# Moving the first block's gated recurrence from stages of its own into the stage of its input projections

## The reference, cut to what matters

```python
u = rmsnorm(h, mix_norm[l])
p = u @ w_mix_in[l]                       # 1024 -> 3712 columns (29 tiles of 128)
p_conv, p_hg, p_rw = jnp.split(p, ...)    # 6, 12 and 11 tiles
y = concatenate([short_conv_mixer(p_conv), hgrn2_mixer(p_hg), rwkv7_mixer(p_rw)])
```

```python
b = cumsum(log_f)                         # inside a chunk
o_inter = (q * exp(b)) @ state            # what came before the chunk
att[t, s] = sum_d q[t,d] k[s,d] exp(b[t,d] - b[s,d])   for s <= t
o = o_inter + att @ v
state = exp(b_last) * state + (k * exp(b_last - b)).T @ v
```

## Time and profile before

| | |
|---|---|
| median of 3 runs | 3573.84 us |
| fastest and slowest | 3562.53 and 3575.74 us |
| span of the profiled execution | 3556.9 us |
| time of the profiled execution beside its span | not given apart; the fastest run is 5.6 us, the median 16.9 us above the span |
| TensorE busy | 3365.1 us (95%) |
| VectorE busy | 1915.8 us (54%) |
| ScalarE busy | 1191.7 us (34%) |
| mean granted clock of TensorE | 0.971 |

### The profile page before, as it was taken

The page is one execution under the profiler, slowest core; times in us unless marked ns, Lnnn a source line. Parts: engine busy times, 40 slices in busy tenths (PEclk is TensorE's granted clock), DMA queues, the critical chain, the costliest instruction groups (busy, mean ns, idle before and its releaser), DMA issues. The chain is left out here.

```text
span 3556.9 us, 49475 instructions
## 1 busy us (share of the span) xinstructions
PE 3365.1 (95%) x21386; PEld 2766.5 (78%) x21386; DVE 1915.8 (54%) x2703; ACT 1191.7 (34%) x1678; POOL 5.5 (0%) x6
## 2 busy tenths in 40 slices
PE   7999996799999999999997799999999988999998
PEld 5888885778788888888886778788887857878886
DVE  4434656755454445444647655453456766457475
ACT  3322433134332233223423033332233175334243
POOL 0000000000000000000000000000000000000000
PEclk9999997899999999999996899999999999999999
DMA  3323222014123232323220023122323202323232
GB/s 122 110 85 105 93 89 66 2 52 134 60 95 101 95 101 89 107 89 104 89 88 10 3 67 130 66 95 96 100 95 119 89 1 91 117 72 106 90 99 73
DMA packets 78200, 301.73 MB, mean 85 GB/s; under 512 B 8946, under 2 KB 9586, under 8 KB 77344
## 3 DMA queue, kind: packets, MB, share of 16 engines
q1 hardware_dynamic: 77984, 298.56, 25.4%
HBM read 296.40 MB, written 6.06 MB: 85 GB/s over the span
## 5 line engine op out<-in xcount | busy, mean ns | idle before, releaser
L315 DVE TENSOR_TENSOR w_lo<-ring,w_hi 128x1024 fp32r<-128x1024 f32 (+1 forms) x508 | 652.8, 1286 | 503.1 <-ACT w_hi L308 503.1
L333 PE MATMUL ps<-xa_hi,w_hi 128*128 128x512 f32 x1728 | 686.3, 397 | 14.2 <-DVE w_lo L315 12.6
L334 PE MATMUL ps<-xa_lo,w_hi 128*128 128x512 f32 x1728 | 677.7, 392 | 0.0
L335 PE MATMUL ps<-xa_hi,w_lo 128*128 128x512 f32 x1728 | 677.4, 392 | 0.0
L308 ACT ACTIVATE w_hi<-ring 128x1024 fp32r<-128x1024 f32 (+1 forms) x508 | 554.1, 1099 | 336.4 <-DMA ring<-in_ffn_in_dram 74.7
L333 PE MATMUL ps<-xb_hi,w_hi 128*128 128x512 f32 x1248 | 490.1, 393 | 0.0
L335 PE MATMUL ps<-xb_hi,w_lo 128*128 128x512 f32 x1248 | 486.4, 390 | 0.0
L334 PE MATMUL ps<-xb_lo,w_hi 128*128 128x512 f32 x1248 | 486.3, 390 | 0.0
L333 PEld LDWEIGHTS ps<-xa_hi,w_hi 128*128 128x128 f32 x1728 | 327.1, 189 | 94.0 <-DVE w_lo L315 14.7
L334 PEld LDWEIGHTS ps<-xa_lo,w_hi 128*128 128x128 f32 x1728 | 327.5, 190 | 68.8 <-issue 3.0
L335 PEld LDWEIGHTS ps<-xa_hi,w_lo 128*128 128x128 f32 x1728 | 327.1, 189 | 68.9
(11 more groups left out here) (356 smaller groups left out, 3485.0 us busy)
## 6 DMA issues: line engine op xcount, KB each, us to landing
ring<-in_ffn_in_dram SPq DMA_DIRECT2D x176, 512.0 KB, 3.5
ring<-in_ffn_out_dram SPq DMA_DIRECT2D x64, 704.0 KB, 4.1
ring<-in_mix_in_dram SPq DMA_DIRECT2D x58, 512.0 KB, 3.5
ring<-in_up_dram SPq DMA_DIRECT2D x44, 512.0 KB, 3.5
ring<-in_w_in_dram SPq DMA_DIRECT2D x22, 512.0 KB, 3.5
ring<-in_down_dram SPq DMA_DIRECT2D x16, 704.0 KB, 4.1
ring<-in_mix_out_dram SPq DMA_DIRECT2D x16, 512.0 KB, 3.6
ring<-in_xk_dram SPq DMA_DIRECT2D x16, 512.0 KB, 3.4
```

The source lines that it names most:

```text
L315: dve.tensor_tensor(core.w_lo[j][:, 0:width], core.ring[j][:, 0:width], core.w_hi[j][:, 0:width].bitcast(F32), ALU.subtract).then_inc(self ...
L333: pe.matmul(out, hi, x_hi, start=(opens and k == tiles[0]), stop=False)
L334: pe.matmul(out, hi, x_lo, start=False, stop=False)
L335: last = pe.matmul(out, lo, x_hi, start=False, stop=(closes and k == tiles[-1]))
```

## The change

The three stages of `hgrn` are gone. Their work is put into steps 9 to 26 of the projection stage, by a class `Recurrence` whose `tensor`, `scalar` and `vector` are called at the end of each step, on banks 4 to 7 alone. Its buffers `u[6]` to `u[8]` lie where the ring's slots 3 and 4 lay; the projection blocks use only slots 0 to 2, are split two steps ahead, and use banks 0 to 2; bank 3 takes the three low-rank products, one before each of the projections 23, 24 and 25. The order of the tiles is forget, query, input, convolution, gate. The level buffers are two in place of three. The memset of the picked matrix is on GpSimd. The outputs from the states accumulate onto those from inside the chunks in PSUM, without chunk 0, whose state is zero. The convolution moves to steps 16 to 22 and works in place. The copy of two tiles of y moves to the start of `rwkv`, and so does, in layer 0, the DMA of the bias rows. The small weights `g2` are loaded early in the projection stage.

```diff
-ORDER = [*range(HF, HF + 3), *range(CONV0, CONV0 + 6), *range(HQ, HQ + 3), *range(HI, HG + 3), RWA, RG,
+ORDER = [*range(HF, HF + 3), *range(HQ, HQ + 3), *range(HI, HI + 3), *range(CONV0, CONV0 + 6), *range(HG, HG + 3), RWA, RG,
          *range(RK, RK + 3), *range(RR, RR + 3), *range(RV, RV + 3)]
...
 class Stream:
     def add(self, part):
         part.first = len(self.plan)
-        self.plan += part.blocks
+        for block in part.blocks:
+            last = {j: max((n for n, at in enumerate(self.slot) if at == j), default=j - RING) for j in range(part.slots)}
+            j = min(last, key=last.get)
+            self.before.append(last[j])
+            self.slot.append(j)
+            self.plan.append(block)
...
 class MixIn(Project):
+    slots, AHEAD, LORA = 3, 2, 3
...
     def sync(self, sp, n):
...
+        if n == self.first + 4:
+            sp.wait_ge(self.phase["used"], self.first)
+            sp.dma_start(self.lora_g, self.io["g2"][self.layer]).then_inc(self.phase["lora"], 16)

     def tensor_all(self, pe):
         for i in range(self.n):
-            if i >= 4:
-                pe.wait_ge(ph["projected"], self.base + i - 3)
+            if i >= 3:
+                pe.wait_ge(ph["projected"], self.base + i - 2)
...
+            if 23 <= i < 26:
+                m = i - 23
+                if m == 0:
+                    pe.wait_ge(ph["squashed"], 1)
+                    pe.wait_ge(ph["lora"], 32)
+                else:
+                    pe.wait_ge(ph["opened"], m)
+                pe.matmul(core.ps[:, self.LORA, :], ...).then_inc(ph["low_rank"], 1)
             ph.stream.multiply(pe, self.first + i, KD, self.x, core.ps[:, self.bank(i), :], ready)
             self.rooted(pe, i)
+            self.recurrence.tensor(pe, i)
...
-            self.phase.stream.split_hi(act, self.first + i + LEAD)
+            if i:
+                self.split_hi(act, i + self.AHEAD)
             self.scalar_aside(act, i, link)
+            self.recurrence.scalar(act, i)
...
-        if i == 12:
-            self.projected(act, 11)
+        if i == 9:
+            self.projected(act, 5)
             act.activation(self.q, self.q, ACT.Silu).then_inc(ph["q_silu"], 1)
...
+class Recurrence:
+    TURN_V, TURN_K, SCORES, UPDATES, INSIDE, ACROSS = 9, 10, 11, 12, 24, 25
+
+    def level(self, i):
+        n, late = divmod(i - self.SCORES, 2)
+        return (n, late) if 0 <= n <= len(LEVELS) else (None, None)
+
+    def tensor(self, pe, i):
+        ph, ps = self.phase, self.core.ps
+        if i in (self.TURN_V, self.TURN_K):
...
+            for q in range(4):
+                if n:
+                    pe.wait_ge(ph["h_copied"], q + 1)
+                for m in range(3):
+                    last = pe.transpose(ps[:, 4 + q, m * P:(m + 1) * P], self.moves[n][0][:, m, q * P:(q + 1) * P], ...)
+                last.then_inc(ph["h_turned"], 1)
+        n, late = self.level(i)
+        if n is not None and not late:
+            if n == 0:
+                pe.wait_ge(ph["h_copied"], 8)
+                pe.wait_ge(ph["q_silu"], 1)
+            else:
+                pe.wait_ge(ph["h_formed"], 2 * n)
+                pe.wait_ge(ph["h_picked"], 4 * n)
+            if n == 1:
+                pe.wait_ge(ph["h_taken"], 4)
+            for m, h, c in SYSTEMS:
+                last = pe.matmul(by_head(ps, 4, m, h, c), ...)
+            last.then_inc(ph["h_scored"], 1)
+        if i == self.UPDATES:
+            pe.wait_ge(ph["h_picked"], 4)
+            chunk_updates(pe, ps, ph["h_updated"], self.ke_n, self.v_n, 4)
+        if i == self.INSIDE:
+            pe.wait_ge(ph["h_picked"], 4 * (len(LEVELS) + 1))
...
+        if i == self.ACROSS:
+            pe.wait_ge(ph["h_inside"], 1)
+            for m in range(3):
+                pe.wait_ge(ph["h_carried"], m + 1)
+                for c in range(1, NCH):
+                    for h in range(2):
+                        last = pe.matmul(self.out_at(m, h, c), ..., start=False, ...)
+
+    def scalar(self, act, i):
+        if i in (self.TURN_V, self.TURN_K):
...
+            for q in range(4):
+                act.wait_ge(ph["h_turned"], 4 * n + q + 1)
+                act.activation(self.moves[n][1][:, q, :], ps[:, 4 + q, 0:384], ACT.Copy).then_inc(ph["h_copied"], 1)
+        if i == self.UPDATES + 1:
+            act.wait_ge(ph["h_updated"], 1)
+            take_updates(act, ps, self.kv, ph["h_taken"], 4)
+        n, late = self.level(i)
+        if n is not None and not late and n < len(LEVELS):
+            act.wait_ge(ph["h_gapped"], 2 * (n + 1))
+            act.activation(gap, gap, ACT.Exp).then_inc(ph["h_grown"], 1)
...
+    def vector(self, dve, i, link):
+        n, late = self.level(i)
+        if n is not None and not late:
+            self.pick(dve, n)
+            if n < len(LEVELS):
+                self.differences(dve, n)
+        if n is not None and late and n < len(LEVELS):
+            self.form(dve, n)
+        if i == 22:
...
+        if 22 <= i < 25:
+            dve.tensor_tensor_scan(...).then_inc(ph["h_carried"], 1)
+
+    def blank(self, pool):
+        pool.wait_ge(ph["used"], self.mix.first)
+        pool.memset(self.att, 0.0).then_inc(ph["h_blank"], 1)
...
-def hgrn(core, g2, layer):
...
+            act.activation(core.y[:, 0:2, :], big[:, 0:2, :], ACT.Copy).then_inc(moved, 1)
...
-            hgrn(core, io["g2"], layer)
-            rwkv(core)
+            rwkv(core, layer)
```

More of the change, by code:

```diff
@@ L312, in split_lo @@
             return
[L313 removed]
+        core, j, width = self.core, self.slot[n], self.plan[n][2]
         dve.wait_ge(self.halved, n + 1)
@@ L803, in tensor_all @@
                 self.first_banks(pe, g)
-            slot = (self.first + n) % RING
+            slot = self.phase.stream.slot[self.first + n]
             pe.wait_ge(ph["parted"], self.first + n + 1)
@@ L1962, in att_of, with chunk_updates @@
     return att[half(c % 2), at:at + C]
-def chunk_outputs(pe, ps, done, terms, base=0, tiles=range(3)):
-    for m in tiles:
-        for q in range(NCH // 2):
-            for h, r in CORNERS:
-                (lhs, rhs), = terms(m, h, 2 * q + r)
-                last = pe.matmul(ps[half(h), (base + 2 * m + r) % 8, q * C:(q + 1) * C], lhs, rhs, start=True, stop=True)
-        last.then_inc(done, 1)
-def copy_by_parity(act, ps, m, o, taken, base=0):
-    dst = o[:, m, :].rearrange("p (q r t) -> p r q t", r=2, t=C)
-    bank = (base + 2 * m) % 8
-    act.activation(dst, ps[:, bank:bank + 2, 0:256].rearrange("p r (q t) -> p r q t", t=C), ACT.Copy).then_inc(taken, 1)
-def chunk_updates(pe, ps, done, left, right):
+def chunk_updates(pe, ps, done, left, right, base):
     for m in range(3):
@@ L1998, in take_updates @@
         r, b = divmod(bank, 2)
-        act.activation(dst[:, b, :, r, :], ps[:, bank, 0:384].rearrange("p (q f) -> p q f", q=2),
+        act.activation(dst[:, b, :, r, :], ps[:, base + bank, 0:384].rearrange("p (q f) -> p q f", q=2),
                        ACT.Copy).then_inc(taken, 1)
-def state_outputs(pe, ps, done, state, q, base, tiles):
-    for m in tiles:
-        for c in range(NCH):
-            for h in range(2):
-                last = pe.matmul(ps[half(h), base + m, c * C:(c + 1) * C], state(m, h, c), q(m, h, c), start=True, stop=True)
-        last.then_inc(done, 1)
 def by_parity(ps, m, h, c):
@@ L2016, in by_parity, with rwkv @@
     return ps[half(r), 4 * r + 2 * h + n // 8, n % 8 * C:(n % 8 + 1) * C]
-def rwkv(core):
+def rwkv(core, layer):
     nc, ps, big = core.nc, core.ps, core.big
@@ L2808, in _ @@
             phase.stream.sync(sp, then, select.sync if last else mix.sync)
-            sp.wait_ge(phase["shifted" if last else "lora"], 16 * (HEADS // 2 if last else 1))
+            sp.wait_ge(phase["shifted" if last else "lora"], 16 * (HEADS // 2 if last else 2))
+        if not last:
+            @block.gpsimd
+            def _(pool):
+                mix.recurrence.blank(pool)
         @block.tensor
```

341 lines of the change are left out of this document (164 added, 177 removed).

## The result

The changed kernel takes 3526.0 us in the median of four runs (3521.0 to 3531.7), the kernel before 3568.2 (3560.9 to 3575.7, four runs, the three shown above among them): a ratio of 0.9889, 95% interval 0.9869 to 0.9909. Five more runs on another chip gave 3527.7 and 0.9893 (0.9877 to 0.9910). The forecast was 3526. It is hit more exactly than its sum was: the median of before came down by 5.6 us with the fourth run, so the gain to be explained is 42 us, not 47.9.

A forecast was written before the change was run, and what follows sets the result against it. TensorE was taken to bound the projection stage. Removing 109.9 us and adding 31.0 a layer (products 22.0, waits 8.8, rounding 0.2) gave -47.9, so 3573.8 became 3526 us; range 3512 to 3548.

The forecast's parts named there:

- The ring: Projection stage's weight slots: VectorE may come 3.5 us late; its two-step work, at most 10.3 us, fits TensorE's 12.5.
- The removed 109.9 us: Stretch from `hgrn`'s first matmul to `rwkv`'s first: 55.7 us in layer 0 and 54.2 in layer 1 disappear.
- rival C: Start of `rwkv`: TensorE comes in at full clock, up to 3 us a layer gained, 3520; chance 0.10.
- TensorE's added 22.0 us: Projection stage, per layer: transposes 3.1, score products 11.4, updates and inside outputs 3.3, outputs from the states 4.2.
- The waits, 8.8 us: Projection stage, per layer: TensorE waits for other engines at steps 10, 13, 19, 21, 24 and 25.
- Step 10: Turning ke in the projection stage: TensorE waits 1.4 us for ScalarE's late copies that free the banks.
- step 24: Second low-rank product: TensorE waits 4.3 us, the largest wait, for bank 3, which ScalarE frees with a sigmoid.
- the walk: Step-by-step working of four engine programs through their waits, with old-trace durations; the stage grows by 31.0 us a layer.
- Clock 1.00 in the stage: Projection stage: the added TensorE work is priced at full-clock durations, with no loss to half clock.
- rival B: Clock falls in the projection stage; first case, only after step 24's wait, costs 1 to 2 us a layer, 3529; chance 0.20.
- The second case: Of rival B: all small products in the projection stage run at half clock, 40.5 us a layer, 3545.
- Rivals D and E: Projection stage: D, VectorE becomes the bound, 3599, chance 0.03; E, each level late by half its chain, 3568, chance 0.05.

## Why the prediction was right

**What bounds the stage: right.** TensorE was to set its length, so that the work added to it counts in full. The ring cost nothing (1.1 us, walked and measured), the stage after is 95% TensorE, and doubled products cost what they take, beside the pauses that came with them.

**The removed 109.9 us: right.** Nothing of it came back: before `rwkv` stands one barrier, as before `hgrn`, and its first matmuls still take 5.45 and 5.46 us, so rival C did not happen. The moved y copy lies beneath them, and TensorE waits for no load in the stage. The 1.2 us that `rwkv` is longer in layer 0 go with the clock: up to its chain it ran 43 us at half clock in place of 37.

**TensorE's added 22.0 us: one term mis-sized.** Level products 1.63 for 96, updates and inside 1.63 each, transposes 1.5 and 1.6: as forecast. The outputs from the states took 5.3 instead of 4.2. The bounds were 1.4 to 5.0, and it fell outside. The old row of 5.7 for 96 held no wait to subtract: the 2.1 us beside it stand before it. Nor does full clock make these products cheaper: they took 66 ns each at half clock in layer 0 of the kernel before, 59 where 3.4 of the 5.7 us were at half clock (layer 1), and 63 at full clock now.

**The waits, 8.8 us: right in place.** Step 10 measured 1.36 (forecast 1.4), the levels at 19 and 21 together 1.4 (1.7), step 13 0.3 (0.8), step 24 3.26 (4.3), step 25 0.65 (0.7): 7.0 in sum. The stage has five more table loads than before, where the walk had six.

**Clock 1.00 in the stage: wrong at one place.** This is the term of the sum that was priced at nothing. The first case of rival B happened beside the forecast: behind the pause of step 24, and only there, TensorE fell to half clock, at 3.0 and 1.7 us a layer where 1 to 2 was written. That rival was given 0.20 as an alternative; a pause of the size that the prediction had itself measured as followed by half clock should have been in the sum. The second case, small products at half clock, did not happen in the stage but behind pauses. The Trainium skill ("TensorE: Matmul & The Clock Gate", section "HAM oscillation — how this bites in real kernels") describes a kernel in which the wait before each group of matmuls makes that group start at the low clock. Here half clock came with each pause of 3.26 us (six of them, in three profiles) and with those of 4.5 and 5.5, with four of the six between 1.9 and 2.4, and with no shorter one: not with 1.36 at step 10 nor with 0.65 at step 25. Between 1.9 and 2.4 us the length does not decide it: 2.33 and 2.34 differ above.

The terms together: products +1.1, waits -1.8 and -1.6, the half clock +3.0 and +1.7. What is left of the 35.4 and 34.1 against 31.0 is 2.1 and 1.9, which no one row accounts for; the walk's own end stood 0.4 short of the trace in the kernel before.

**The sum: -47.9 forecast, 40.4 in the stages, 42 between the medians.** 7.5 us of the shortfall is the stage (twice 3.7). The chain over the states, which the prediction did not look at because nothing in it changes, then moves single executions by 7 us a layer either way. It is larger than any term that was disputed, and the three runs of before gave no sure median. By the span the sum forecast 3509, and 3529.9 was measured. That 3526.0 came out to the tenth is luck: two errors of 5.6 and 5.7 us, in the median of before and in the gain, in opposite directions.

**Rivals D and E** did not happen: TensorE met the products of two levels late, by 1.4 us in sum, not of six. The runs with picks twice and with nearly no level products show how near they are.

## What to carry to other kernels

Work bound by VectorE goes well beneath a stage bound by TensorE, and a walk through the engines' programs with durations of the old trace finds its waits, place by place, to about 1 us. Price each pause of TensorE that such a walk finds with what follows it: here 3.3 us idle cost 1.7 to 3.0 more at half clock, and giving each low-rank product two steps took 12.5 us off the two stages. Before a gain of 1% is told from one profiled execution, look in its trace at serial chains that the change does not touch; here one of them is worth 14 us.

## What the runs showed of the hardware that was not expected

- A recorded 64x64 matmul in float32 took 17 ns when 96 went round four corners with contiguous weights, 32 with two corners in turn, and 63 with its weights at a stride of 8 as well (66 at half clock).
- TensorE paused for 0.5 to 2.2 us at a time, with no wait that the profile shows, inside bursts of 192 small products, 6.4 us in one layer. The bursts of 96 between projections show none. Where small products follow on small products such pauses stand in the other profiles too: 1.7 and 1.6 us in the outputs of the kernel before (L1972 and L2008, layer 0), and two or three of 0.6 to 1.9 in the chain over the states, in each layer of every profile. What they are was not found.
- The same serial chain of small products took 34.4 to 36.9 us at full clock (but for up to 3.4 us at its start) and 41.9 to 43.2 where the clock fell 25 us into it, in one execution and not in the next. What decides that was not found, and filler products between its steps did not hold it.
